# Conditioning vector and sums of squares by four 32-column groups of TensorE, VectorE for the first remainders, eight begun tiles, gate sums moved beside attention

## What is computed

```python
# first block
mod = silu(c) @ w_ada + b_ada              # c: 1 x 2048, w_ada: 2048 x 6144
shift, scale, gate = split(mod, 3)
h = rms(x, norm_g) * (1 + scale) + shift   # sums of squares over 2048
proj = h @ w_in                            # 2048 x 8192: four attention parts, four of the HGRN part
x = x + gate * (concat(attention, hgrn2) @ w_out)
# second block
mem_k, mem_v = split(rmsnorm(mem, mem_norm_g) @ w_mem_kv, 2)   # mem: 256 x 2048
... three attentions, gated merge, w_o
```

## Time and profile before

| | |
|---|---|
| runs (3) | 2763.95, 2765.26, 2766.51 us, median 2765.26 |
| the profiled execution | 2765.54 us, span 2764.2 us, granted clock 0.989 |
| busy share | PE 98%, PEld 80%, DVE 38%, ACT 38%, POOL 45% |
| main matmuls of full items, L754 to L756 | 3 x 2928 |
| moved | 323.29 MB, mean 117 GB/s |

### The profile page before, as it was taken

How to read it: one execution, slowest core, us unless ns; L and a number is a source line. 1 busy time by engine, 2 the same in 40 slices (tenths; PEclk the granted TensorE clock), 3 DMA queues, 4 the chain that set the end, 5 groups by cost and what they waited for, 6 DMA issues and landing times.

```text
span 2764.2 us, 31580 instructions
## 1 busy us (share of the span) xinstructions
PE 2714.6 (98%) x12680; PEld 2208.8 (80%) x12680; DVE 1046.2 (38%) x1570; ACT 1043.0 (38%) x1678; POOL 1245.8 (45%) x631
## 2 busy tenths in 40 slices
PE   7999999999999999999999999999999999999999
PEld 5878888887787888878888777777888888888787
DVE  5856755644112113134467333334232233212300
ACT  4224333334334333234443444444444344333311
POOL 3634333434433445453334444444555455545543
PEclk9789999999999999999999999999999999999999
DMA  9843323322222223432222222332333333333443
GB/s 364 287 165 141 115 107 115 115 77 73 81 88 92 80 88 128 147 126 84 77 77 84 92 95 96 103 103 96 107 103 110 111 105 120 118 113 116 135 138 111
DMA packets 102097, 323.29 MB, mean 117 GB/s; under 512 B 11328, under 2 KB 12864, under 8 KB 101440
## 3 DMA queue, kind: packets, MB, share of 16 engines
q1 hardware_dynamic: 98208, 307.64, 32.3%
q10 hardware_dynamic: 3744, 13.63, 1.3%
HBM read 304.45 MB, written 16.78 MB: 116 GB/s over the span
## 4 chain that ended last, share of the span: by engine, by line
PE 87%; DVE 6%; DMA 2%; ACT 1%; POOL 1%; issue 1%; SPq 0%; DVEq 0%; ACTq 0%
PE bank L754 25%; PE bank L756 25%; PE bank L755 25%; PE bank L876 2%; DVE TA L1782 2%; PE bank L953 1%; POOL wlo L1999 1%; DVE TA L1477 1%; PE bank L942 1%; PE bank L804 1%; DMA TA<-in_strip 1%; PE bank L936 1%; ACT whi L1058 1%; PE bank L907 1%; PE bank L704 1%
## 5 line engine op out<-in xcount | busy, mean ns | idle before, releaser
L1999 POOL TENSOR_TENSOR wlo<-wraw,whi 128x1024 fp32r<-128x1024 f32 (+2 forms) x454 | 1050.4, 2315 | 1341.3 <-ACT whi L1058 1340.6
L754 PE MATMUL bank<-Hhi,whi 128*128 128x512 f32 x2928 | 1196.7, 409 | 8.9 <-DVE Hlo L1974 3.5
L756 PE MATMUL bank<-Hhi,wlo 128*128 128x512 f32 x2928 | 1145.7, 391 | 0.0
L755 PE MATMUL bank<-Hlo,whi 128*128 128x512 f32 x2928 | 1145.6, 391 | 0.0
L1058 ACT ACTIVATE whi<-wraw 128x1024 fp32r<-128x1024 f32 (+2 forms) x454 | 456.8, 1007 | 701.6 <-PE bank L756 668.3
L754 PEld LDWEIGHTS bank<-Hhi,whi 128*128 128x128 f32 x2928 | 552.3, 189 | 146.5 <-issue 24.7
L755 PEld LDWEIGHTS bank<-Hlo,whi 128*128 128x128 f32 x2928 | 552.6, 189 | 118.7 <-issue 10.8
L756 PEld LDWEIGHTS bank<-Hhi,wlo 128*128 128x128 f32 x2928 | 551.4, 188 | 119.2
L754 PE MATMUL bank<-Ohi,whi 128*128 128x512 f32 x320 | 128.0, 400 | 0.0
L756 PE MATMUL bank<-Ohi,wlo 128*128 128x512 f32 x320 | 124.8, 390 | 0.0
L755 PE MATMUL bank<-Olo,whi 128*128 128x512 f32 x320 | 124.7, 390 | 0.0
(11 more groups left out here) (256 smaller groups left out, 2620.6 us busy)
## 6 DMA issues: line engine op xcount, KB each, us to landing
wraw<-in_w_in SPq DMA_DIRECT2D x304, 512.0 KB, 3.2
TA<-in_w_ada SPq DMA_DIRECT2D x64, 512.0 KB, 5.8
Y<-in_w_ada SPq DMA_DIRECT2D x32, 512.0 KB, 4.4
wraw<-in_w_out SPq DMA_DIRECT2D x32, 512.0 KB, 3.2
wraw<-in_w_o SPq DMA_DIRECT2D x32, 512.0 KB, 3.2
wraw<-in_w_mem ACTq DMA_DIRECT2D x16, 512.0 KB, 6.7
tmp_mgs<-TA SPq DMA_DIRECT2D x32, 256.0 KB, 2.3
TA<-tmp_mgs SPq DMA_DIRECT2D x32, 256.0 KB, 3.5
```

The lines of the kernel that those rows point to most:

```text
L754: e.matmul(out, hi[:, c], xhi[k], start=first and j == 0, stop=False)
L755: e.matmul(out, hi[:, c], xlo[k], start=False, stop=False)
L756: m = e.matmul(out, lo[:, c], xhi[k], start=False, stop=last and end)
L1999: e.tensor_tensor(M.wlo[b][:, 0:w], M.wraw[b][:, 0:w], M.whi[b][:, 0:w].bitcast(F32), ALU.subtract).then_inc(S.lo)
```

## The change

- The conditioning: all 64 pieces go to TensorE, four at a time. `ada(q)` takes pieces 4q to 4q+3; each of the four has a stationary tile of 32 equal columns (`c32`) and writes 32 partitions of a bank, for two banks of 512 outputs: eight matmuls of 512 columns, 16 such visits in all. ACT copies the two banks to SBUF once for a chunk (`ada_rows`), and `sums` adds up the four groups with eight one-column matmuls by `sel` as before. VectorE's 43 multiply-and-adds are gone, as are the 21 x 8 one-column matmuls of L704. There are eight places for pieces, refilled in fours.
- Sums of squares: four pieces at a time in the same manner (`groups`), four visits for the memory tokens (256 columns) and four for x (512 columns); ACT copies the result out, and one full matmul by ones (x) or two one-column matmuls by `sel` (memory) add up the groups.
- Memory tokens: the gain is applied inside the copy to the high part (ACT) and inside the remainder (VectorE), so VectorE's 16 separate multiplications are gone.
- The low parts of the first 24 weight items, of all memory pieces and of all pieces of h are made by VectorE; POOL starts with item 24.
- The LOW pieces of h are no longer made two by two in the last four memory items but in one go after them.
- Eight tiles are begun in place of six, and the two new ones use the banks that the conditioning is added up in, so their start waits for ACT's copy (`adr`) and for the final addition (`adp`).
- The gate's 32 pieces move from beside the HGRN heads to beside attention, into other memory; the two transposes of the memory keys move behind the first HGRN head.

The core of the diff:

```diff
-BEGUN = (48, 33, 40, 32, 56, 41)
 CHUNKS = (2, 0, 3, 1)
-PLACES = 6
+PLACES = 8
+START = [(x[0], int(x[1:])) for x in "m0 m1 a0 m2 m3 a1 m4 m5 m6 a2 m7 m8 a3 m9 m10 s0 a4 m11 m12 a5 m13 a6 a7 m14 s1 m15".split()]
+BEGUN = ((48, 3, ()), (41, 2, (8,)), (56, 4, (9,)), (33, 5, (10,)), (49, 1, (11,)), (57, 0, (12, 13)), (40, 7, (14, 15)),
+         (32, 6, ()))
...
-        self.xr = self.xsq[0]
+        self.xr = self.rows
         self.rr, self.kss, self.krr = self.par[:, 93:95], self.small[:, 40:48], self.small[:, 48:56]
-        self.masks_in = TA[:, 8192:9216]
...
+        self.masks_in = first[:, 1024:2048]
+        self.ada_slot, self.c32 = pieces(TA, 0, PLACES, 1024), TA[:, 8192:8704]
+        self.ada_rows = (first[:, 0:1024], first[:, 3072:4096])
+        self.sel = self.par[:, 105:106]
+        self.gate_slot = (first[:, 0:1024], first[:, 1024:2048], first[:, 3072:4096])
+        self.gate_acc = first[:, 4096:5120]
...
-    for k in range(KT):
-        do["mem"](k)
+    for what, i in START:
+        do[{"m": "mem", "a": "ada", "s": "sums"}[what]](i)
     beat.add("core", do["mem_kv"]())
-    begun = {}
-    for n, (tile, bank) in enumerate(zip(BEGUN, (BS0, BST, beat.open(), beat.open(), BS1, BT))):
-        begun[tile] = bank
-        if n < 4:
-            do["ada"](range(48 + 4 * n, 52 + 4 * n))
-        if n == 5:
-            do["h_gain"](1)
+    do["gain"](0)
+    do["h_put"](LOW)
+    for tile, bank, fours in BEGUN:
+        for i in fours:
+            do["ada"](i)
+        if tile == BEGUN[-1][0]:
+            do["sums"](2)
+            do["sums"](3)
+            do["gain"](1)
             do["h_put"](HIGH)
         do["part"]("h", LOW, bank, True, False)
-    beat.drain("core")
-    do["masks"]()
-    beat.add("slow", do["gates"]())
+    begun = {tile: bank for tile, bank, _ in BEGUN}
...
+                if h == 0:
+                    beat.add("slow", do["mem_turn"]())
...
+    beat.add("slow", do["gates"]())
...
+    def groups(out, ones32, pieces, start, stop):
+        for g, (w, x) in enumerate(zip(ones32, pieces)):
+            m = e.matmul(out[32 * g:32 * g + 32, :], w, x, start=start, stop=stop, skip_group_check=True)
+        return m
     def mem(k):
         i = beat.item
         hi, lo = M.whi[i % NRING], M.wlo[i % NRING]
         xhi, xlo = M.pair["mem"]
-        pe.wait_ge(S.msq, k + 1)
-        for tt in range(2):
-            m = e.matmul(M.bST[:, tt:tt + 1], M.mem_sq[k % 8][:, tt * P:(tt + 1) * P], ones[:, 0:1],
-                         start=k == 0 and tt == 0, stop=k == KT - 1, skip_group_check=True)
-        m.then_inc(S.mst)
+        same = [ones[:, 0:32]] * 4
+        if k in (2, 4, 6, 8):
+            q = k // 2 - 1
+            pe.wait_ge(S.msq, 4 * q + 4)
+            groups(M.bST[:, 0:256], same, [M.mem_sq[(4 * q + g) % 8] for g in range(4)], q == 0,
+                   q == 3).then_inc(S.mst)
+        if k == 9:
+            pe.wait_ge(S.mrow, 1)
+            for tt in range(2):
+                m = e.matmul(M.bST[:, 300 + tt:301 + tt], M.mem_sq[0][:, 0:256][:, tt * P:(tt + 1) * P], M.sel,
+                             start=False, stop=True, skip_group_check=True)
+            m.then_inc(S.mst)
+        if k in (5, 7, 9, 11):
+            q = (k - 5) // 2
+            pe.wait_ge(S.xsq, 4 * q + 4)
+            groups(M.bS0, same, M.xsq, q == 0, q == 3).then_inc(S.xst)
+        if k == 12:
+            pe.wait_ge(S.xrow, 1)
+            e.matmul(M.bS0, ones, M.xsq[1], start=True, stop=True).then_inc(S.xst)
...
-        if k < 8:
-            for x in (2 * k, 2 * k + 1):
-                pe.wait_ge(S.xsq, x + 1)
-                e.matmul(M.bS0, ones, M.xsq[x % 4], start=x == 0, stop=x == KT - 1).then_inc(S.xst)
-        ada(range(3 * k, 3 * k + 3))
-        if k == 6:
-            totals(0)
-        if k == 11:
-            totals(1)
-        if k >= 12:
-            h_put((2 * k - 24, 2 * k - 23))
         beat.done("mem", [])
         if k == KT - 1:
-            free[BS0], free[BST] = (S.xr, 1), (S.rr, 1)
+            free[BS0], free[BST] = (S.xr, 1), (S.adp, 2)
             free.update({bank: (S.mkv, n + 1) for n, bank in enumerate(MEM_BANKS)})
-            free[BVV] = (S.adp, 2)
-    def ada(pieces):
-        for a in pieces:
-            if by_tensor(a):
-                half, c = a // 32, a // 16 % 2
-                pe.wait_ge(S.ada[a % PLACES], 16 * (a // PLACES + 1))
-                pe.wait_ge(S.setv, 8)
-                for i in range(8):
-                    at = 8 * c + i
-                    m = e.matmul((M.bV, M.bO)[half][:, at:at + 1], M.ada_slot[a % PLACES][:, i * P:(i + 1) * P],
-                                 M.par[:, 64 + a % 16:65 + a % 16], start=a in (2, 32) and i == 0, stop=False,
-                                 skip_group_check=True)
-                m.then_inc(S.adq)
-    def totals(chunk):
-        pe.wait_ge(S.adm, taken(16 * chunk + 15, False))
+            free[BVV], free[BO] = (S.adr, 4), (S.adp, 4)
+    def ada(q):
+        places = [(4 * q + g) % PLACES for g in range(4)]
+        pe.wait_ge(S.c32, 2)
+        pe.wait_ge(S.adr, q // 4)
+        for place in places:
+            pe.wait_ge(S.ada[place], 16 * (q // 2 + 1))
+        cs = [M.c32[:, 32 * (4 * q + g) % 512:32 * (4 * q + g) % 512 + 32] for g in range(4)]
+        for half, bank in enumerate((M.bO, M.bV)):
+            m = groups(bank, cs, [M.ada_slot[place][:, half * T:(half + 1) * T] for place in places], q % 4 == 0,
+                       q % 4 == 3)
+        m.then_inc(S.adq)
...
+    def sums(chunk):
+        pe.wait_ge(S.adr, 4 if chunk > 1 else chunk + 1)
+        pe.wait_ge(S.rr, 1)
+        out, at = (M.bST, 256) if chunk < 2 else (M.bO, 0)
         for i in range(8):
-            at = 8 * (chunk % 2) + i
-            m = e.matmul((M.bV, M.bO)[chunk // 2][:, at:at + 1], M.ada_acc[chunk % 2][:, i * P:(i + 1) * P],
-                         ones[:, 0:1], start=False, stop=True, skip_group_check=True)
+            c = at + 8 * (chunk % 2) + i
+            m = e.matmul(out[:, c:c + 1], M.ada_rows[chunk % 2][:, i * P:(i + 1) * P], M.sel,
+                         start=chunk == 2 and i == 0, stop=True, skip_group_check=True)
         m.then_inc(S.adc)
...
+    def ada(q):
+        if q % 4 == 3:
+            chunk = q // 4
+            act.wait_ge(S.adq, q + 1)
+            act.wait_ge(S.plv, KT)
+            act.wait_ge(S.adc, chunk - 1)
+            e.activation(M.ada_rows[chunk % 2], M.ada_sum, ACT.Copy).then_inc(S.adr)
...
+    def rest_of(j):
+        if j < FIRST_RESTS:
+            b, w = j % NRING, ITEMS[j][3]
+            dve.wait_ge(S.hi, j + 1)
+            e.tensor_tensor(M.wlo[b][:, 0:w], M.wraw[b][:, 0:w], M.whi[b][:, 0:w].bitcast(F32),
+                            ALU.subtract).then_inc(S.lo)
...
+        dve.wait_ge(S.phi, k + 1)
+        e.scalar_tensor_tensor(out=M.pair["mem"][1][k], in0=M.memt[k], scalar=M.c("mem_g", k, 1),
+                               in1=M.pair["mem"][0][k].bitcast(F32), op0=ALU.mult, op1=ALU.subtract).then_inc(S.plv)
+        n.up("plv")
     def mem(k):
-        if k < 8:
-            mem_gain(k + 8)
-        ada(range(3 * k, 3 * k + 3))
-        if k < 8:
-            mem_rest(k + 8)
-        elif k < 12:
-            for x in (4 * k - 31, 4 * k - 29):
-                dve.wait_ge(S.xr, 2)
-                e.tensor_tensor(M.y[x], M.y[x], M.xr, ALU.mult).then_inc(S.xnv)
-        else:
-            if k == 12:
-                h_gain(0)
-            h_put((2 * k - 24, 2 * k - 23))
+        rest_of(beat.item + 2)
+        if k < 6:
+            mem_rest(2 * k + 4)
+            mem_rest(2 * k + 5)
+        if k >= 13:
+            normed(4 * k - 52)
...
+        def scaled(k):
+            dve.wait_ge(S.xn, k + 1)
             e.tensor_scalar(M.y[k], M.y[k], M.par[:, 16 + k:17 + k], M.par[:, k:k + 1], ALU.mult,
                             ALU.add).then_inc(S.hs)
+        scaled(ks[0])
         for k in ks:
-            put("h", k, "y", k, None, on_vector(k))
+            if k < ks[-1]:
+                scaled(k + 1)
+            put("h", k, "y", k, None, True)
...
+        if FIRST_RESTS <= j < len(ITEMS):
             b, w = j % NRING, ITEMS[j][3]
+            pool.wait_ge(S.lo, FIRST_RESTS)
...
+            if a == 44:
+                sp.wait_ge(S.plv, KT)
                 e.dma_start(M.masks_in.bitcast(I32), io["masks"]).then_inc(S.mask, 16)
-            if a >= PLACES:
-                sp.wait_ge(S.adq if by_tensor(a) else S.adm, taken(a - PLACES, by_tensor(a)))
+            sp.wait_ge(S.adq, a // 4 - 1)```

How it moves instructions, at three places. TensorE, end of the second memory item (cst holds the ones, par the conditioning input, TA the `w_ada` pieces). Before:

```order
L676 MATMUL bank5<-wlo1,Hhi 128x512
L681 MATMUL bank3<-first,cst 128x512 x2
L704 MATMUL bank7<-par,TA 128x1 x8
L665 MATMUL bank2<-cst,first 128x1 x2
L674 MATMUL bank1<-whi2,Hhi 128x512
```

(47 more changed lines are left out.)

174 lines of the change are left out of this document (66 added, 108 removed).

## The result

The changed kernel takes 2751.61 us (median, 2750.56 to 2753.7) against 2765.26 before: ratio 0.9951, 95% interval 0.9936 to 0.9965, 13.7 us faster. Forecast were 2745, with 2728 to 2762 as the range. The profiled execution of the changed kernel has a span of 2750.3 us, 13.9 under that of before.

The account below looks back on a forecast made before the run. TensorE's queue was taken as the path. The opening wins 22 us, the HGRN stage 1, attention loses 3: -20 from the profiled 2765.5, forecast 2745, range 2728 to 2762.

Parts of the forecast that it names:

- The mark: Start of the first HIGH half with eight tiles begun: at 185 us against 207.2 before, 22 us won.
- Waits: PE's waits in the opening, for VectorE, transfers and begun tiles together: 25 us, bounds 15 and 35.
- the 3.3 for VectorE's pace: At the LOW pieces VectorE makes one in 1.1 us and PE eats one in 0.69: 3.3 us of waits.
- The clock: PE's lower clock in the opening: a quarter of the 27 us lost before remains, 7 us, bounds 2 and 24.
- rivals 4 and 5: Conditioning visits: groups in program order, 4.2 us each, 2775 (7 in 100); groups in turn, 6.8 + 0.36, 2819 (3 in 100).
- The LOW pieces in one go: After the last memory item PE waits 3.5 us for VectorE, which then makes a piece in 1.1 us.
- VectorE's gains cost nothing except in one place: VectorE's added remainders (34 us) and low parts (13) in the opening cost nothing except at the LOW pieces.
- Transfers: Opening: PE waits 15.4 us in all for loads, at the first two visits, close later visits and begun tiles.
- The HGRN stage: Taking the gate pieces away from beside the HGRN heads wins 1 us (0 to 3).
- Attention: Beside attention about one gate piece a head falls into the softmax chain: 3 us lost (0 to 10).
- Rival 2: Attention gives back: gate pieces push PE by a full 1.3 us each, 13 lost, 2755; 10 in 100.
- the prediction's own signs of being wrong: A mark over 200 us, or a gain at the mark that is gone at the end of attention.

Follow-up runs that it names:

- experiment 8: The changed kernel with weight remainders 2 to 23 made on POOL again in place of VectorE; ratio 0.9931 to the kernel before.
- experiment 3: The changed kernel with the four loads of x issued behind the first eight conditioning pieces rather than among them; ratio 0.9952 to the kernel before.
- experiment 7: The changed kernel with the x squares added up by full 128-column matmuls again; ratio 0.9977 to the kernel before.

## Why the prediction was right, and where it was not

- *The mark.* Forecast 185 us, measured 184.8, by terms that are mostly right and some luck. The visit holds: measured as the prediction measured it, from the last matmul ahead to the second one behind, 131.61 to 134.13, less two plain intervals of 0.23, it is 2.06 us for 2.07. Of that 1.85 lies from start to start, the rest in the two matmuls at its edges. The x and memory squares come out the same way at 1.19 and 0.76, for 1.22 and 0.79. Start 12.2, not 14.0: the remainder on VectorE takes 1.23 us. Waits 25.7 (20.0, 4.1, 1.2, 0.4) against 25: a sum that came out by luck, since the transfers were 5 too low and the rest 4 too high (the 3.3 for VectorE's pace is in no wait). The clock: 0.90, 0.93, 0.93, 0.93 in the four stretches are 31 us at the lower level. In some 10 of these PE stood still and lost nothing:

```profile
21.90:28.60 6.70, 0.00 (x0) 0.01 (x1) 2.87 (x6) 2.69 (x6) 0.00 (x0) 0.51 1.02 413
28.60:32.40 3.80, 3.78 (x21) 1.11 (x24) 0.00 (x0) 0.00 (x0) 0.00 (x0) 0.51 1.01 410
...
90.00:92.90 2.90, 0.01 (x2) 0.04 (x3) 0.00 (x0) 0.00 (x0) 0.00 (x0) 0.56 0.91 343
92.90:97.30 4.40, 4.40 (x18) 1.38 (x19) 0.00 (x0) 0.71 (x1) 0.00 (x0) 0.51 0.86 349
...
108.40:114.30 5.90, 5.85 (x14) 4.62 (x15) 5.90 (x12) 3.37 (x6) 0.00 (x0) 0.50 0.00 0
...
175.50:182.60 7.10, 6.68 (x19) 5.28 (x19) 6.24 (x15) 3.34 (x6) 0.00 (x0) 0.52 0.00 0
```

The other 21 cost about 10, where the forecast took 7. So the clock gave back some 17 of the 27 us that it cost before, more than the 14 that PE's own work shrank by (56.5 to 42). Both together are more than the 22 won; the longer waits took the difference. That the column groups are what brought the clock back is likely, but no run changes them alone.
- *The groups beside each other.* Right; rivals 4 and 5 are out. The strict order of starts that the Trainium skill ("TensorE: Matmul & The Clock Gate", Part 3) states does not make the two records of a float32 matmul a chain here: 1.85 us is what four at a time give, 4.2 would be the chain. Its factor of 3.07, which it gives for four row tiles, would be 2.2 us for a visit, an estimate; the trace has 6.84 / 1.85 = 3.7 for four column groups, or 3.3 with the edges in (2.06).
- *The LOW pieces in one go.* Forecast a wait of 3.5, measured 4.1, and a piece every 1.06 us where 1.1 was taken. I took it as the price of spreading less; experiment 8 shows that a remainder in front of it, which waits for ACT, makes most of the wait (4.1 to 1.4), and that the step "VectorE's gains cost nothing except in one place" had the right place and the wrong reason.
- *Transfers.* The 15.4 us of waits were 20.0, and they lie elsewhere: 9.3 at the first visit, whose pieces came at 28.6 us and not near 22, for 2; 1.1 at the second for 4.4; 9.6 at four later ones for 9. By experiment 3 it was x in the queue that held the first visit (22.2 with x behind), and moving it gains nothing in all. By experiment 7 more PE work shows in full.
- *The HGRN stage.* Forecast 1 us, measured 5.6. I left out that the two gate additions leave this stage and arrive in attention, 3.5 us each way.
- *Attention.* This is the step that failed, and the total came into the range in spite of it: "about one gate piece a head falls into it, 1.3 to 1.7 us each less the slack: 3 us lost (0 to 10)". Measured 15.4, or 12 without the additions, above the bound. I counted a piece's own duration and took the waits of L936 as a small leftover. In truth they were the mark of a chain without slack, started by a strip that came late: the trace of before has 92.4 us of VectorE's waits for strips, at all eight heads, and the prediction leaves them out. A gate piece there costs itself, what POOL does to the instruction behind it (twice a wait of 3.7 us came of it), and the clock behind the wait. Nor is it one piece a head: four heads have one in the chain and make 10.8 of the 13.0 us. Rival 2 had the place and a price of 13, close to what came, and I gave it 10 in 100. The total, 2745 against 2751.6, is off by less than this term's 12.4, because the HGRN stage won 4.6 more than forecast and the opening 1.9 more. That is partly luck: 3.5 of the 4.6 are the additions, the same 3.5 that are part of attention's 15.4. And of the prediction's own signs of being wrong, a gain at the mark that is gone at the end of attention, half came true.

## What to carry to other kernels

Before side work is moved to a stage because its engine has room there, look at what that engine waits for in front of the chain it serves: an engine that stands still for a late load and then works in a row has room on average and none where it counts. Bringing the load forward (here one edit on the SP queue) was worth as much in the changed kernel as the whole change, and 8 us in the kernel before. And cost a moved step in both stages, with its matmuls, not only with the engine that had the most of it.
